# Products that nobody reads in TensorE's waits, the forget gates moved into the middle of K, and the merge's low halves all on GpSimd

## The reference

```python
h = _rms(x, attn_norm_g)
fq, fk, fv = proj("fox_q"), proj("fox_k"), proj("fox_v")       # each 1024 x 1024
log_f = log_sigmoid(proj("fox_f") + b_forget)                  # 1024 x 16: the forget gates
cum_f = cumsum(log_f)        # enters the attention's logits as cum_f[q] - cum_f[k]
y_fox = fox_attention(_rms(fq), _rms(fk), fv, log_f)
branches = stack([y_fox, y_lru, y_sb, y_mem])                  # four branches
gates = sigmoid(proj("gates") + b_gate)
mixed = sum_n(gates[n] * (branches[n] @ w_branch[n]))          # the merge
x = x + mixed @ w_out;  x = x + conv_swiglu(_rms(x))           # FFN, w_up and w_down
```

## Time and profile before

| | us |
|---|---|
| median of 3 runs | 2955.91 (2947.69 to 2959.1) |
| the profiled execution's own time | 2956.62 |
| its span, first to last instruction | 2954.8 |
| TensorE busy | 2573.3 (87%) |
| DVE / ACT / GpSimd busy | 1077.0 / 884.7 / 347.1 |
| mean granted TensorE clock | 0.957 |

### The profile page before, as it was taken

One profiled execution on the slowest core, in us unless ns is written; L12 is line 12 of the kernel. 1 busy time (PEld: TensorE's weight loads), 2 busy tenths in 40 slices (PEclk: granted clock), 3 DMA queues, 4 the chain that ended last, 5 costly groups with the idle time before them and its releaser, 6 DMA issues. The chain is left out here.

```text
span 2954.8 us, 37912 instructions
## 1 busy us (share of the span) xinstructions
PE 2573.3 (87%) x15018; PEld 1799.9 (61%) x15018; DVE 1077.0 (36%) x1556; ACT 884.7 (30%) x1398; POOL 347.1 (12%) x185
## 2 busy tenths in 40 slices
PE   7899989999999999899987888887898987788786
PEld 7788877889997678688742222224776982222222
DVE  4447533446754434543430011014455651000001
ACT  4465533344443343422320000002334441000001
POOL 0330003341000221000310000000132020000000
PEclk8999999999999999999989999998998999999999
DMA  4434326664543121322279999996212457999996
GB/s 179 149 133 160 115 86 258 265 224 168 185 157 129 72 68 45 155 100 100 100 282 407 400 405 411 414 407 247 100 59 81 172 219 298 411 393 411 410 409 278
DMA packets 92888, 669.31 MB, mean 227 GB/s; under 512 B 10288, under 2 KB 10464, under 8 KB 12736
## 3 DMA queue, kind: packets, MB, share of 16 engines
q1 hardware_dynamic: 90256, 654.63, 56.9%
q0 software_dynamic: 2208, 11.43, 1.1%
q10 hardware_dynamic: 272, 1.05, 0.1%
HBM read 666.00 MB, written 1.06 MB: 226 GB/s over the span
## 5 line engine op out<-in xcount | busy, mean ns | idle before, releaser
L2429 PE MATMUL ps<-ring,WK 128*64 128x512 f32 x2984 | 703.9, 602 | 151.7 <-DMA ring<-in_stream 128.2
L562 PE MATMUL ps<-A,piece_hi 128*128 128x256 f32 (+1 forms) x1952 | 624.0, 320 | 39.2 <-DVE ring_lo L481 10.9
L563 PE MATMUL ps<-A,piece_hi 128*128 128x256 f32 (+1 forms) x1952 | 610.0, 313 | 0.0
L564 PE MATMUL ps<-A,ring_lo 128*128 128x256 f32 (+1 forms) x1952 | 609.3, 312 | 0.0
L2429 PEld LDWEIGHTS ps<-ring,WK 128*64 128x64 f32 x2984 | 189.3, 136 | 630.6 <-DMA ring<-in_stream 330.0
L481 DVE TENSOR_TENSOR ring_lo<-ring,piece_hi 128x1024 fp32r<-128x1024 f32 x287 | 355.7, 1244 | 381.2 <-ACT piece_hi L472 380.7
L472 ACT ACTIVATE piece_hi<-ring 128x1024 fp32r<-128x1024 f32 x378 | 391.5, 1053 | 265.0 <-DMA ring<-in_stream 120.2
L562 PEld LDWEIGHTS ps<-A,piece_hi 128*128 128x128 f32 x1952 | 382.4, 196 | 82.7 <-issue 48.9
L563 PEld LDWEIGHTS ps<-A,piece_hi 128*128 128x128 f32 x1952 | 382.8, 196 | 18.3
L564 PEld LDWEIGHTS ps<-A,ring_lo 128*128 128x128 f32 x1952 | 381.7, 196 | 18.6
L483 POOL TENSOR_TENSOR ring_lo<-ring,piece_hi 128x1024 fp32r<-128x1024 f32 x91 | 235.8, 2596 | 791.1 <-ACT piece_hi L472 791.1
(11 more groups left out here) (271 smaller groups left out, 2683.6 us busy)
## 6 DMA issues: line engine op xcount, KB each, us to landing
ring<-in_stream SPq DMA_DIRECT2D x610, 1024.0 KB, 7.6
WK<-in_ahead SPq DMA_DIRECT2D x5, 1024.0 KB, 9.2
WK<-in_na_bias POOLq DMA_DIRECT2D x2, 2048.0 KB, 7.8
hi_place<-in_ahead SPq DMA_DIRECT2D x4, 1024.0 KB, 12.8
WK<-cum_scratch POOLq DMA_DIRECT2D x1, 2048.0 KB, 11.7
A_place<-in_ahead SPq DMA_DIRECT2D x2, 1024.0 KB, 17.2
const<-in_const SPq DMA_DIRECT2D x1, 1235.0 KB, 10.5
WK<-in_x SPq DMA_DIRECT2D x1, 1024.0 KB, 5.2
```

The lines of the kernel that those rows point to most:

```text
L562: nc.tensor.matmul(out_, l[0], r[0], start=first, stop=False)
L563: nc.tensor.matmul(out_, l[0], r[1], start=False, stop=False)
L564: return nc.tensor.matmul(out_, l[1], r[0], start=False, stop=last)
L2429: last = nc.tensor.matmul(ps[64 * n:64 * n + 64, bank, :], lhs, piece[:, n * 512:n * 512 + 512], start=(k == 0), stop=(k == DC - 1))
```

## The change

Three things:

1. `idle_products` makes matmuls of two constants (128x128 by 128x256 float32) into a PSUM bank that is free; nobody reads the result. 88 of them are put ahead of waits of TensorE: 2 or 3 ahead of the wait for 1/rms, 5 ahead of the first normed tile (`first_banks`), 2 to 3 ahead of seven stage edges, 3 more behind the edge to the turned context and 4 behind the turn, and 4 to 8 ahead of the first or last softmax wait of four attentions.
2. The forget gates' product, its bias and its activations go into the middle of K (behind 4 of its 8 banks).
3. In the first block's merge all 64 low halves are GpSimd's instead of 32.

```diff
-    for lo, hi in ((24, 40), *((block + l * layer + 12, block + l * layer + 32) for l in range(LAYERS)),
+    for lo, hi in ((24, 40), (88, 152), *((block + l * layer + 12, block + l * layer + 32) for l in range(LAYERS)),
                    (block + 32, block + 35)):
         GPS_LOW[split[lo:hi]] = True
-    GPS_LOW[split[89:152:2]] = True
...
+        def idle_products(pe, n, out_):
+            for _ in range(n):
+                nc.tensor.matmul(out_, ident, const[:, 0:2 * P], start=True, stop=True)
+        def idle_bank(pe, cur, n):
+            b, used = cur.next_bank()
+            if used:
+                pe.wait_ge(bank_free[b], used)
+            idle_products(pe, n, ps[:, b, 0:2 * P])
...
             def turn(r, j):
                 t = t_of(r, nk)
-                pe.wait_ge(att_probs, CREDIT + base + r + 1)
                 pe.wait_ge(att_copied, CREDIT + cbase + r * len(chunks) + j)
                 if at["y_bank"] < 6:
                     pe.wait_ge(att_saved, CREDIT + base + r)
+                if j == 0 and r in (0, n - 1):
+                    idle_products(pe, idle_n[r > 0], ps[:, 4, 0:2 * P])
+                pe.wait_ge(att_probs, CREDIT + base + r + 1)
...
+            idle_products(pe, 2 if n > T else 3, ps[:, b, 0:2 * P])
             pe.wait_ge(rstd_ready, cur.base("rstd") + 1)
...
+            idle_products(pe, 5, ps[:, cur.bank(gs[0]), 0:2 * P])
             for k in range(DC):
                 ready(k)
...
-            fm_banks(pe, cur, in_a()(T), T, DC)
+            fm_banks(pe, cur, in_a()(T), T, DC // 2)
+            forget_pe(pe, cur)
+            fm_banks(pe, cur, in_a()(T), T, DC // 2)
...
-            for h in range(2):
-                copies(eng, who, cur, lambda j, h=h: KT[:, 4 * h + j, :], 4, T)
+            behind()
+            copies(eng, who, cur, lambda j: KT[:, j, :], 4, T)
+            forget()
+            copies(eng, who, cur, lambda j: KT[:, 4 + j, :], 2, T)
+            gates()
+            copies(eng, who, cur, lambda j: KT[:, 6 + j, :], 2, T)
...
+            idle_bank(pe, cur, 2)
             barrier(pe, cur)
             cur.set_ring((6, 7))
             fox_pe(pe, cur, lambda i: fm_banks(pe, cur, in_a()(T), T, 1))
+            idle_bank(pe, cur, 2)
             barrier(pe, cur)
...
+            idle_bank(pe, cur, 3)
             barrier(pe, cur)
+            idle_bank(pe, cur, 3)
             pe.wait_ge(loads, 16 * LOADS["ctx"])
             turn_in_pe(pe, cur, CTX_TM, range(2))
+            idle_bank(pe, cur, 4)
             down_pe(pe, cur)
...
-                att_pe(pe, cur, na_x[layer], also=lambda i: (proj3_pe(pe, cur, i, n), value_pe(pe, cur, i, n) if n == T else None))
+                att_pe(pe, cur, na_x[layer], also=lambda i: (proj3_pe(pe, cur, i, n), value_pe(pe, cur, i, n) if n == T else None),
+                       idle_n=(5 if n > T else 8, 0))
...
-                att_pe(pe, cur, da_x[layer], also=lambda i: gated_pe(pe, cur, i, n // P))
+                att_pe(pe, cur, da_x[layer], also=lambda i: gated_pe(pe, cur, i, n // P), idle_n=(4, 5))
```

More of the change, by code:

```diff
@@ L235, in set_ring, with next_bank @@
         self.ring, self.turn = list(banks), 0
+    def next_bank(self):
+        if self.g < len(self.places):
+            return self.places[self.g]
+        b = self.ring[self.turn % len(self.ring)]
+        return b, self.uses[b]
     def used(self, bank):
@@ L717, in att_chunks, with att_pe @@
             return [[0, 1]] if at["nk"] == 256 else [[0], [1]]
-        def att_pe(pe, cur, at, also=lambda slot: None):
+        def att_pe(pe, cur, at, also=lambda slot: None, idle_n=(0, 0)):
             nk, n, per = at["nk"], at["n"], at["per"]
@@ L1258, in qk_pe, with qk_read @@
             fm_banks(pe, cur, in_a()(T), T, DC - 3)
-            fm_banks(pe, cur, in_a()(T), T, DC)
+            fm_banks(pe, cur, in_a()(T), T, DC // 2)
+            forget_pe(pe, cur)
+            fm_banks(pe, cur, in_a()(T), T, DC // 2)
         def v_pe(pe, cur, kv=0):
             tm_tile(pe, cur, kv, TT)
-        def qk_read(eng, who, cur, beside):
+        def qk_read(eng, who, cur, beside, behind, forget, gates):
             for c in range(DC):
@@ L1294, in forget_dve, with gates_dve @@
             dve.drain().then_inc(fox_z, 1)
+        def gates_dve(dve, steps):
             dve.wait_ge(fox_e, 1)
@@ L2655, in _ @@
             qk_pe(pe, cur, ready=norm_ready(pe, cur, 2 * T, streams=1))
-            forget_pe(pe, cur)
             head_norm_pe(pe, cur, fox_norm, 4, lambda j: tm_piece(pe, cur, 0, TT, j),
@@ L2742, in _ @@
             main_norm_act(act, cur, steps, 2 * T, streams=1)
[L2743 to L2747, removed]
+            qk_read(act, "act", cur, beside=lambda c: norm_hi_act(act, cur, c, 1, None, True), behind=lambda: None,
+                    forget=lambda: skip_banks(cur, 1), gates=lambda: forget_act(act, cur, steps))
+            qk_written(act, cur)
             act.wait_ge(x_lo, cur.base("x"))
-            head_norm_act(act, cur, steps, fox_norm, after_squares=lambda: forget_act(act, cur, steps),
+            head_norm_act(act, cur, steps, fox_norm,
                           ahead=lambda: v_read(act, "act", cur, 0), between=lambda: next_piece(act, cur, 2),
@@ L2851, in _ @@
             main_norm_dve(dve, cur, steps, 2 * T, gain, streams=1, between=first_lows)
-            qk_read(dve, "dve", cur, beside=lambda c: second_chunk_dve(dve, cur, c, gain, None))
-            second_chunk_dve(dve, cur, DC, gain, None)
-            forget_dve(dve, cur, steps)
+            qk_read(dve, "dve", cur, beside=lambda c: second_chunk_dve(dve, cur, c, gain, None),
+                    behind=lambda: second_chunk_dve(dve, cur, DC, gain, None),
+                    forget=lambda: forget_dve(dve, cur, steps), gates=lambda: gates_dve(dve, steps))
             head_norm_dve(dve, cur, steps, fox_norm, ahead=lambda: v_read(dve, "dve", cur, 0),
```

## The result

The changed kernel took 2926.44 us (median of 4, 2916.89 to 2933.68) beside 2957.27 us for the kernel before (median of 4). The ratio is 0.9906, with a 95% interval of 0.9883 to 0.9929: clear of no change. Forecast were 2934 us, a range of 2916 to 2951, and "faster by over 0.5%" with a chance of 0.66.

What follows compares the result with a forecast made beforehand. TensorE, busy 87% of the span, was taken as the bound, losing time in waits and at half clock. Forget gates -11, merge -5 and products -7 sum to -23, from 2956.6 to 2934 us; range 2916 to 2951.

Steps and rivals of the forecast that it cites:

- A: Whole kernel: the forecast itself, all three parts gain in part, 2934 us, own range 2924 to 2944; chance 0.50.
- Forget gates: Fox attention edge: gates' chain ends 10 us earlier, plus 1 us of half clock; -11 us, bounds -14.6 and -6.
- Merge: First block's merge: moving all low halves to GpSimd gains 5 us; bounds -9.6 and +15.
- (a): Merge: GpSimd takes 2.48 us per low half against DVE's 1.23, so 1.25 us could come on top at each.
- (b): Merge: without its low half DVE reports pieces used earlier, so the next load leaves up to 1.25 us earlier.
- shorter waits may save that, for which I take nothing: Merge: the clock falls behind the two ROWS waits; shorter waits might avoid it, but no gain was counted.
- D: Merge: shared port makes every y-half sum wait for a GpSimd instruction; +15 instead of -5, 2954 us; chance 0.08.
- Products: TensorE's waits: products win back 15 us of half-clock loss and cost 8; net -7 us, bounds -44 and +9.
- half of 30: Stretches at waits given products: 30 us lost to the half clock, of which 15 was taken as regained.
- rival B: Half-clock stretches at placed waits: clock comes back nearly everywhere, 30 us instead of 15, 2919 us; chance 0.14.
- Rival C: Products buy nothing: clock falls move to other waits and the cost of 8 stays, 2949 us; chance 0.22.
- E: Products are not hidden: each paid in full, 38 us instead of 8, no clock gain, 2978 us; chance 0.06.

Runs made afterwards that it cites:

- e2: Kernel before with only the change that gives all 64 low halves of the first merge to GpSimd: 2944.04 us, ratio 0.9958.
- e3: Kernel before with only the 88 products added: 2947.44 us, ratio 0.9974.
- e10: Changed kernel with none of the 88 products, forget gates and low halves as changed: 2933.97 us, ratio 0.9937.
- e13: Changed kernel run again, unchanged: 2924.74 us, ratio 0.9890.
- e1: Kernel before with only the forget gates moved into the middle of K: 2949.84 us, ratio 0.9990, same within the measurement.
- e9: Changed kernel with the three low halves behind GpSimd's mask steps at the fox edge given to VectorE: 2926.25 us, ratio 0.9906.
- e6: Kernel before with three more low halves on GpSimd, those ahead of the first merge's copies to ROWS: 2953.36 us, ratio 0.9994.
- e12: Changed kernel with products re-placed by measured waits: more at the memory attention and gated branch edges, fewer at norms and context: 2914.55 us, ratio 0.9859.
- e7: Changed kernel with only the 32 products at the norms kept: 2936.26 us, ratio 0.9942.
- e11: Changed kernel without the norms' 32 products, keeping the 56 at edges, context and attentions: 2921.73 us, ratio 0.9881.
- e5: Changed kernel with each of the 88 products made twice: 2948.66 us, ratio 0.9980.

## Why the prediction was right, and where its sizes were off

**Rival or forecast.** The case that came is A: each part gains where it acts, and the sum lands 8 us below 2934. The merge's term was clearly too small (5 forecast; 11.4 us in its stage, 10.5 in e2's medians), the forget gates' too large, and the products' near what the medians show (7.1 in e3, 9.2 from e10 to e13) but too small by the stages.

**Forget gates, -11 forecast, -8.8 (e1) and -7.4 (with the products) in the stage.** The chain did what was worked out: the store leaves at 86.83 in the changed kernel, forecast 86.6, and the mask steps begin 11.2 us earlier (106.14 against 117.36). The step that was off is "GpSimd is through at 133.6 - 10.0 = 123.6": it was through at 125.6. Moved 11 us forward, the mask steps lie beside VectorE's copy and low half of the head norm, and the four took 12.50 us instead of 9.30. The other half of the timeline is VectorE's, in the changed kernel:

```profile
106.14 12.50 POOL L1344 TENSOR_TENSOR WK<-WK,const 128x1024 f32<-128x1024 f32 x4 [14.95 <-DMA WK<-cum_scratch]
```

```profile
107.39 3.30 DVE L1253 COPY WK<-hvar 128x4096 f32<-128x4096 f32 x1
110.61 3.40 DVE L487 TENSOR_TENSOR ring_lo<-ring,piece_hi 128x1024 fp32r<-128x1024 f32 x1
113.93 4.78 DVE L1265 SCALAR_TENSOR_TENSOR WK<-WK,par,ps 128x256 f32<-128x256 f32 x12
```

and the same three in the kernel before, where GpSimd did nothing at that time:

```profile
107.06 2.29 DVE L1231 COPY WK<-hvar 128x4096 f32<-128x4096 f32 x1
109.27 1.22 DVE L481 TENSOR_TENSOR ring_lo<-ring,piece_hi 128x1024 fp32r<-128x1024 f32 x1
111.68 4.79 DVE L1243 SCALAR_TENSOR_TENSOR WK<-WK,par,ps 128x256 f32<-128x256 f32 x12 [1.20 <-PE ps L575]
```

Both engines pay: GpSimd 3.2 us, VectorE 1.0 on the copy and 2.2 on the low half. Taken one by one, the second and third mask steps show who waited for what:

```profile
108.50 4.42 POOL L1344 TENSOR_TENSOR WK<-WK,const 128x1024 f32<-128x1024 f32 x1
```

```profile
112.89 3.38 POOL L1344 TENSOR_TENSOR WK<-WK,const 128x1024 f32<-128x1024 f32 x1
```

Alone a step took 2.33 to 2.40 us. The second is longer by 2.1 us, about the copy's 2.29, the third by 1.0, about the low half's 1.22: the two engines take turns, and each instruction waits for the other's to end. In e1 a further low half fell beside the first step and the four took 13.55 us, in e9 two further ones fell beside them and they took 14.13: 0.6 to 1.1 us more for each. The twelve scaling steps that read a PSUM bank pay nothing (4.78 and 4.79). The Trainium skill ("SBUF — State Buffer", Who interferes with whom) gives the rule: a VectorE instruction with two SBUF inputs contends with a GpSimd instruction that reads SBUF, a copy can contend (in the modes that use both ports), whichever comes first keeps the shared ports for its whole length, and a VectorE instruction with at most one SBUF input outside those modes does not contend. The trace agrees, with the numbers above. The prediction used that page on the merge and not here, where GpSimd's work was moved onto VectorE's.

**Merge, -5 forecast, -11.4 in the changed kernel, -7.2 (e2) and -13.3 (e10).** The direction of (a) and (b) was right, the waits for ROWS did go. Mis-sized was the sentence "shorter waits may save that, for which I take nothing": with the two waits the half clock behind them went, and the merge's matmuls are 7.9 us less busy. e6 shows that the two belong together: without the waits for ROWS the two stretches are gone, and the matmuls are 5.8 us less busy. The waits themselves gave 3.5 us, near the -5, but in part by luck, for two errors cancel. The ROWS waits went whole (4.9 us, 2.4 forecast), while the halves, forecast to win 2.4 us, lost 1.3: TensorE waited 8.6 us for low halves of both engines before and 9.9 for GpSimd's after. The prediction's "DVE's even halves were just in time" was a misreading: TensorE had waited for them 9 times, 3.9 us in all. The rival D, that the sums wait for a GpSimd instruction each, is refuted by the merge, which got shorter, and by the sum's own row in the changed kernel (ns, min/median/max): some are blocked, up to 2.5 us, but the median fell from 666 to 503.

```profile
L1822 DVE TENSOR_TENSOR WK<-WK x32: 424/503/2529, 435.5 to 644.1; 128x256 f32<-128x256 f32 x32
```

The blocking that D is built on is there, but it costs less than D took. 12 of the 32 sums stand where no half of GpSimd runs and take 0.42 to 0.43 us, and one that meets a half waits only for what is left of it. Here the half ends at 446.59 and the sum at 446.87:

```profile
444.22 2.37 POOL L489 TENSOR_TENSOR ring_lo<-ring,piece_hi 128x1024 fp32r<-128x1024 f32 x1 [3.13 <-ACT piece_hi L478]
445.31 1.56 DVE L1822 TENSOR_TENSOR WK<-WK 128x256 f32<-128x256 f32 x1
```

**Products, -7 forecast.** From e10 to e13 the medians fall by 9.2 us, and by 19.5 outside the streams. The clock's part was sized too low: busy time at the half clock falls from 188.6 (e10) to 136.5 us (e13), which at 45% is 24 us, where half of 30 was taken. Whether the cost was sized too high or too low depends on which gain is taken: 24 - 19.5 = 4.5 us by the stages outside the streams, 24 - 9.2 = 15 us by the medians, against 8. One of its items was dearer here than forecast (0.45 us, at the full clock): at the norm behind the merge the three products fell into the half clock and the spread to all partitions starts 2.6 us behind the drain (670.93) instead of 0.83 (695.10 to 695.93), 1.8 us late:

```profile
670.99 2.73 PE L576 MATMUL ps<-const 128*128 128x256 f32 x6 [0.94 <-ACTq L465]
673.51 0.63 PE L1042 MATMUL ps<-const,nvar 128*128 128x128 f32 x2
```

With two products there (e12), at the full clock, it starts 0.97 us behind the first of them, not 2.52. Another item was not there: behind the edge to the context the 3 and 4 products lie in the wait for the split tiles, of which 0.82 us was still left:

```profile
815.01 0.36 PE L568 MATMUL ps<-WKR,piece_hi 128*128 128x256 f32 x1 [0.82 <-DVE WKR L688]
```

The argument for rival B ("every one of the 13 stretches starts at or right behind a placed wait") held for the edges: the stretch of 830.92 is gone (3.4 us of it in e13), that of 906.01 is 3.4 us instead of 10.2. It did not hold for the norms, by e7 and e11. The stretches at 698 and 2425, forecast as short or gone, are still there (671 and 678; 2402).

**The checks.** The wait at the fox edge, forecast 3, was 3.9 us with GpSimd last; waits for 1/rms vanished; the mean clock rose from 0.957 to 0.972, forecast 0.5 to 1.5 points. The half-clock total did not stay and the merge was not longer. Rival C (products buy nothing) is refuted by e10 against e13, whose intervals, 0.9913 to 0.9962 and 0.9867 to 0.9912, do not overlap (by a hair; their single runs do not overlap either); E (nothing hidden) by the same, though e5 shows its mechanism from twice the number on.

**What stays open.** The products' gain is 19.5 us outside the streams but 9.2 in the medians. The streams took 957.0 us in the profile of e10 and 972.6 in that of e13; over the kernels with the full products at edges they took 964 to 975, over those without any 957 to 970. Whether that is chance or the streams give a part back was not settled. The largest single piece of the 19.5, 5.1 us, lies in the stage right ahead of the first stream (83.1 us in e10, 78.0 in e13), and that stream then took 10.2 us more (481.8 and 492.0). Open too is how much of the forget gates' 8.8 us reaches the end (e1: -7 to +1.5 us).

## What to carry to other kernels

Count a wait of a busy TensorE twice: once for its length, and once for the half clock that it may leave behind it; here, at the copies to ROWS, 4.9 us of wait stood beside 5.8 us of busy time lost to the clock. Products that nobody reads paid at edges and in attentions: 56 of 88 did all the good that could be told, twice as many cost 22 us, and dropping or moving some by the measured waits gave 10 us more, though not at every wait that was filled. When work of GpSimd is moved in time, look at what VectorE does at the new place: here copies and two-operand work in SBUF cost both engines, and scaling steps that read PSUM did not.

## What the runs showed of the hardware that I had not expected

- Four mask steps of GpSimd take 9.30 us alone, and took 12.50, 13.55 and 14.13 us (changed, e1, e9) when VectorE's copy and one, two or three of its low halves lay beside them.
- Waits as short as 1.86 us (the kernel before, for a half of GpSimd), 2.2 to 2.7 us (for ROWS), 2.46 us (e6) and 3.12 us (e2) in the midst of dense split products went with a half-clock stretch of 3.4 to 6.8 us. One of 1.80 us in e6 had none, nor had any of up to 1.1 us inside the changed kernel's merge.
- More work in the waits did not end all half clock: doubled products left 180 us of it, single ones 158 to 168.
- The two expert streams, with the DMA engines 98% busy or more in all profiles, vary by 18 us in sum (957.0 to 974.7) between executions, more than most single edits here are worth.
